# Two units of dense work moved ahead of transposes on TensorE in a two-block network

## What is computed

```
# first block, even layer
p   = modulate(x) @ w_in             # dq, dk, dv, gates, mk, mq, mo, mv
h_m = mlstm_mixer(...)               # scans over the gate rows, then h * sigmoid(o)
h_d = diff_mixer(...)                # 4 heads, softmax(s1) - lam * softmax(s2)
x   = x + gt_m * rmsnorm(concat(h_m, h_d) @ w_out)
x   = x + gt_f * rmsnorm(swiglu(modulate(x)))
# first block, odd layer
x   = x + gt_m * rmsnorm(conv_module(modulate(x)) @ pw2_w + pw2_b)
x   = x + gt_f * rmsnorm(moe_swiglu(modulate(x), router_w, w1, w3, w2))   # 8 experts, top 2
# second block, two layers
k, v = split(mem @ w_kv[i])          # the memory's keys and values
... gating / short conv, memory attention, w_out, layer norm, 16 experts in 4 groups
```

## Time and profile before

| | |
|---|---|
| median of 3 runs | 2243.79 us (2243.3, 2243.79, 2245.4) |
| profiled execution, its span on the page | 2243.4 us |
| PE busy | 2059.8 us (92%) |
| DVE, ACT, POOL busy | 496.3, 367.6, 116.4 us |
| share of the chain that ended last | PE 76%, DMA 11%, SPq 5%, DVE 4%, issue 2%, ACT 2% |
| read from memory | 641 MB, 286 GB/s over the span |

### The profile page before, as it was taken

One profiled execution on the slowest core, in us unless ns is written; L12 is line 12 of the kernel. 1 busy time (PEld: TensorE's weight loads), 2 busy tenths in 40 slices (PEclk: granted clock), 3 DMA queues, 4 the chain that ended last, 5 costly groups with the idle time before them and its releaser, 6 DMA issues.

```text
span 2243.4 us, 30002 instructions
## 1 busy us (share of the span) xinstructions
PE 2059.8 (92%) x12470; PEld 1004.1 (45%) x12470; DVE 496.3 (22%) x1255; ACT 367.6 (16%) x845; POOL 116.4 (5%) x275
## 2 busy tenths in 40 slices
PE   5989999999999989999999999959799978979995
PEld 2574547777677343322222222226443326643331
DVE  2143851000159320010000001021401113241113
ACT  2022432000332331000100010013111002111111
POOL 2000000000000100000000000000000000000010
PEclk9999999999999999999999999979899999979998
DMA  9241449442673578999999999982599995089995
GB/s 330 77 150 42 147 178 350 141 155 94 244 256 109 208 301 335 408 412 398 402 402 408 411 398 412 412 338 68 209 388 421 422 403 188 31 335 423 421 415 243
DMA packets 192025, 644.26 MB, mean 287 GB/s; under 512 B 11635, under 2 KB 44875, under 8 KB 156043
## 3 DMA queue, kind: packets, MB, share of 16 engines
q1 hardware_dynamic: 165440, 469.92, 55.0%
q0 software_dynamic: 25824, 172.09, 18.8%
q10 hardware_dynamic: 619, 0.23, 0.0%
HBM read 641.15 MB, written 1.05 MB: 286 GB/s over the span
## 4 chain that ended last, share of the span: by engine, by line
PE 76%; DMA 11%; SPq 5%; DVE 4%; issue 2%; ACT 2%; DVEq 0%; ACTq 0%; POOLq 0%
PE bank L1369 12%; PE bank L970 12%; PE bank L981 9%; PE bank L1406 9%; PE bank L1352 8%; PE bank L1277 7%; DMA ring<-in_l_moe_w 6%; SPq L762 5%; PE bank L1288 3%; DMA ring<-in_w_up 3%; PE bank L1325 3%; PE bank L1437 2%; PE bank L1594 1%; PE bank L1313 1%; DMA ring<-in_l_mod_w 1%
## 5 line engine op out<-in xcount | busy, mean ns | idle before, releaser
L1369 PE MATMUL bank<-ring,wide 128*32 128x512 f32 x3520 | 413.0, 599 | 23.8 <-DMA ring<-in_l_moe_w 22.1
L1406 PE MATMUL bank<-dreg,RB 128*32 128x512 f32 x2592 | 314.9, 605 | 9.5 <-DMA dreg<-in_l_moe_w 4.2
L1369 PEld LDWEIGHTS bank<-ring,wide 128*32 128x32 f32 x3520 | 108.5, 110 | 277.9 <-issue 247.9
L1352 PE MATMUL bank<-ring,wide 128*32 128x512 f32 x1408 | 173.8, 616 | 19.9 <-DMA ring<-in_w_up 18.5
L981 PE MATMUL bank<-wide,ring 128*128 128x256 f32 x832 | 183.5, 382 | 0.6 <-ACT wide L1856 0.6
L3005 DVE TENSOR_TENSOR H<-SG,bank 128x256 f32<-128x256 f32 x82 | 34.7, 423 | 659.3 <-ACT SG L2087 659.3
L981 PEld LDWEIGHTS bank<-wide,ring 128*128 128x128 f32 x832 | 159.0, 192 | 23.3 <-issue 1.3
L1406 PEld LDWEIGHTS bank<-dreg,RB 128*32 128x32 f32 x2592 | 79.6, 111 | 193.0 <-issue 184.5
L970 PE MATMUL bank<-ring,wide 128*128 128x512 f32 x352 | 157.1, 602 | 1.2 <-DMA ring<-in_w_kv 1.0
L1277 PE MATMUL bank<-wide,ring 128*128 128x256 f32 x704 | 153.6, 379 | 0.8 <-DVE MODX L2518 0.8
L1277 PEld LDWEIGHTS bank<-wide,ring 128*128 128x128 f32 x704 | 133.7, 190 | 23.0 <-issue 4.3
(11 more groups left out here) (444 smaller groups left out, 1608.8 us busy)
## 6 DMA issues: line engine op xcount, KB each, us to landing
ring<-in_l_moe_w SPq DMA_DIRECT2D x120, 1024.0 KB, 16.6
dreg<-in_l_moe_w POOLq DMA_DIRECT2D x88, 1024.0 KB, 8.6
dreg<-in_w_down POOLq DMA_DIRECT2D x64, 1024.0 KB, 12.0
ring<-in_w_gate SPq DMA_DIRECT2D x56, 1024.0 KB, 11.9
ring<-in_w_up SPq DMA_DIRECT2D x56, 1024.0 KB, 16.7
ring<-in_l_mod_w SPq DMA_DIRECT2D x24, 2048.0 KB, 8.4
ring<-in_l_moe_w SPq DMA_DIRECT2D x40, 768.0 KB, 12.3
ring<-in_l_ffn_w SPq DMA_DIRECT2D x22, 1024.0 KB, 10.4
```

The costliest lines, as they stand in the source:

```text
L1352: mm = pe.matmul(banks[r % 2][32 * g:32 * g + 32, :].rearrange("p (w n) -> p w n", w=2), tokens_of(m.order[i][0], c, k), w, start=k == 0, ...
L1369: mm = pe.matmul(banks[r % 3][32 * g:32 * g + 32, :].rearrange("p (w n) -> p w n", w=2), tokens_of(m.order[i][0], c, k), quads[:, s, :, k ...
L1406: mm = pe.matmul(banks[4 + 2 * m.lane(m.unit(m.order[i][0])) + h][32 * g:32 * g + 32, :], HQ[:, r % 4, j, 32 * q:32 * q + 32], dring[:, i ...
```

## The change

At the first place `unit_beside(0)`, which makes `mo0`, stands ahead of the wait for the gate rows and of their transposes. At the second, both modulation jobs stand first, then `kv1v1`, then the transposes of the tokens, and then both turns. The list of banks follows: `mo0` and `gT` change places, and so do `kv1v1` and the two turns. No instruction is added or removed.

```diff
-    names += ["dqT0", "dqT1", "dkT0", "dkT1", "gT"] + BESIDE[:1]
+    names += ["dqT0", "dqT1", "dkT0", "dkT1"] + BESIDE[:1] + ["gT"]
...
-    names += lagged(GAP5) + ["kv1v1", "part1", "rt1", "pos1", "cnt1"]
+    names += GAP5 + ["kv1v1"] + [f"{f}T" for f in GAP5] + ["part1", "rt1", "pos1", "cnt1"]
...
+            unit_beside(0)
             pe.wait_ge(sem("gate_rows"), 1)
             o = bank_for("gT")
             for s in range(4):
...
             filled(m, "gT")
-            unit_beside(0)
             pe.wait_ge(sem("diff_operands"), 1)
...
-            mod_jobs(GAP5)
+            for f in GAP5:
+                mod_job(f)
             tok_unit("kv1v1", memT, 1, w_kv)
             turn_normed(XN, 6)
+            for f in GAP5:
+                mod_turn(f)
```

More of the change, by code:

```diff
@@ L1116, in _ @@
                     filled(m, f"d{n}T{b}")
[L1118 to L1124, removed]
             beside = {}
@@ L1137, in _ @@
             unit_beside(0)
+            pe.wait_ge(sem("gate_rows"), 1)
+            o = bank_for("gT")
+            for s in range(4):
+                pe.transpose(o[:, s * GR:(s + 1) * GR], gG[:, s * P:(s + 1) * P], ident[0:GR, 0:GR])
+            for t in range(TT):
+                m = pe.transpose(o[:, (4 + t) * GR:(5 + t) * GR], gE[:, t * P:(t + 1) * P], ident[0:GR, 0:GR])
+            filled(m, "gT")
             pe.wait_ge(sem("diff_operands"), 1)
```

## The result

| | before | with the change |
|---|---|---|
| median | 2244.09 us (4 runs, 2243.3 to 2245.4) | 2230.52 us (4 runs, 2228.38 to 2232.55) |
| profiled execution, its span | 2243.4 us | 2226.8 us (its time 2228.38) |
| ratio | | 0.9931 [0.9919, 0.9943], or -15.5 us (-18.2 to -12.8) |

The kernel is faster by 0.6 to 0.7%. About 1.6 us of an execution's time lie outside its span (2228.38 less 2226.8). The spans differ by 16.6 us, more than the medians (13.6), since the execution shown of the change is its fastest, 2.1 us under its median, and that of before, with the same 1.6 us added to its span, would be at 2245.0, 0.9 above its own.

What follows compares the result with a forecast made beforehand. PE's own list was taken to bound the kernel to about 890 us, then expert loads until near 1460. Terms of 5.5 and 7.3 us made 12.8, so 2243.8 - 12.8 = 2231.0 us, range 2227.5 to 2236.5.

Steps and rivals of the forecast that it cites:

- Term 1: First mixer: `mo0` starts after ACT's first copy at full clock, so scores begin 5.5 us sooner (bounds 4.1 to 5.8).
- Term 2: Ahead of the experts: earlier `kv1v1` and token transposes, turns under ACT's evictions, save 7.3 us (bounds 6.8 to 7.7).
- The sum: Whole kernel: 5.5 + 7.3 = 12.8 us saved from the median of 2243.8 us, giving 2231.0 us.
- DVE and POOL: Ahead of the sort: DVE's gate rows end by 787.5, router's result near 788.7; POOL's constants keep some 2 us.
- The loads: Ahead of the experts: six loads on SP go at about 781.6 instead of 789.17 but land no sooner.
- Rival B: Ahead of the experts: late loads make PE stand until the old time, so 2238.3 us; 7%.
- D: Expert stage, 890 to 1460 us: changed load alternation lowers the DMA rate, time past 2248.3 us; 2%.
- E: Expert stage: a pace not set by PE loses the gain in part or whole, near 2243.8 us; 4%.
- Rival A: First mixer: the clock falls all the same, `mo0` takes 2.1 to 2.3 us more, 2233.3 us; 15%.
- Rival C: Gather ahead of the experts: its clock shifts, up to 3 us less (2228) or as much more (2234); 10%.

Runs made afterwards that it cites:

- both_again: The change once more, unaltered, beside runs of the kernel before: median 2232.08 us, ratio 0.9941.
- p1_only: The kernel before with only the first place changed (`mo0` ahead of the gate rows' transposes): 2239.91 us, ratio 0.9972.
- turns_first: The change with both modulation turns directly behind `kv1v1`, ahead of the tokens' transposes: 2232.90 us, ratio 0.9946 to before.
- turns_last: The change with both modulation turns behind the router instead of behind the tokens' transposes: 2235.79 us, ratio 0.9950 to before.
- p2_only: The kernel before with only the second place changed (`kv1v1` and the tokens' transposes ahead of both turns): 2237.51 us, ratio 0.9959.
- p2_filled: The kernel before with seven unused matmuls between the two modulation turns, no wait removed: 2243.99 us, ratio 0.9990.
- held: The change with unused matmuls in PE's waits, including ahead of `mo0`, their number cut to fit each wait: 2223.38 us, ratio 0.9903 to before.

## Why the prediction was right

The forecast was 2231.0 us; the medians of the change are 2230.52 and, in `both_again`, 2232.08.

- **Term 1**, 5.5 us forecast, 5.6 in the profile, and 6.3 (3.8 to 8.5) over the runs of `p1_only`. `mo0` was to start at 163.65 and started at 163.64: bank 1 did wait for ACT's first copy alone. The transposes behind it took 0.4 us and not 0.7, which is the 0.2 us that the scores (forecast 171.4, measured 171.17) came sooner.
- **Term 2**, 7.3 us forecast, 7.5 at the tokens' transposes and 7.1 at the first expert matmul, the difference being the gather's 7.11 us against 6.71. In PE's timeline the last router step starts 5.1 us behind the transposes' start (774.36 to 779.46), and so it did before (788.98 to 794.08): the turns lie wholly beneath ACT's evictions, and the 0.2 that the term allowed for them was not needed. The prediction lets half of `kv1v1` run at the lower clock before; by windows of the trace the clock was at half from 779.5 to about 782.9, which is 1.3 us of `kv1v1`. The sum doesn't use it. `turns_first` shows the cover by taking it away.
- **DVE and POOL.** DVE's room was put at some 1.2 us (787.5 to 788.7) and was 1.27. POOL's was put at "some 2 us" and is 2.0 to the sort; in `turns_last` it was DVE whose lateness the sort waited for.
- **The loads.** The six loads went out with the start of the tokens' transposes, in an unbroken row on SP:

```profile
774.55 47.68 SPq L762 DMA_DIRECT2D ring<-in_l_moe_w  x14
```

  They were asked for 14.6 us sooner than before (789.17), but the DMA engines were busy all along (share 1.00 to 1.03 in every window of 770 to 798) and ran out of work only near 799.7 (0.86 from 798 to 800), before near 807.2 (0.61 from 806 to 808). Those 7.5 us are about the lead of 7.1 with which the stage began, so in the times of the old trace these loads land hardly sooner, as forecast. PE waits for none of them at the first expert matmuls. Rival B fell, and D and E with it: the stage kept its length (701.5 against 702.0 us) and its rate.
- **Rival A** (15%) is real as a mechanism and rare: seen in the execution of `p1_only`, at 1.4 us, under the 2.1 to 2.3 that it was given. The clock fell ahead of `mo0` there too (0.76 from 164.5 to 165.0, 0.50 behind), but it was back in 168.0 to 168.5 (0.83), after 2.9 us of `mo0`; in the execution of before it was back in 171.5 to 172.0 (0.61), after 4.1. What the prediction said for and against this rival rests on a misreading. The 4.07 us of "issue" from 155.28 are a step of the chain at which DVE waited, not PE. PE's timeline and DVE's, of before:

```profile
154.78 4.48 PE L981 MATMUL bank<-wide,ring 128*128 128x256 f32 x20
```

```profile
159.36 0.88 DVE L2601 TENSOR_SCALAR wide<-bank,PCOL 128x256 f32<-128x256 f32 x2 [4.08 <-issue]
```

  PE started 20 matmuls in that time without a gap, so the clock at 1.00 in 155 to 159 says nothing of a wait, and PE had not "done little since 155.28". The Trainium skill ("TensorE: Matmul & The Clock Gate", Part 1) says that the window is free-running, so that the same kernel changes level at other moments; this agrees with an equal list that kept 1.00 in one execution and fell to 0.72 in another, the stretch being 1.65 us later, and with the two executions of the change itself at 580 us (1.00, and 0.50 in `both_again`).
- **Rival C** (10%) shows in the profiles, as part of the runs' spread. The gather took 7.11 us (the change), 6.97 (`both_again`), 6.72 (`turns_first`), 5.53 (`p2_only`) and 5.91 (`p2_filled`) with the same list at that point, and 3.78 with the clock held.
- **What the sum missed.** The spans differ by 16.6 us and not 12.8. At the first expert matmul the lead is 14.2 us: 5.6 and 7.1 from the two places, and 1.5 from the clock at the second mixer's transposes in the execution of before. The other 2.4 come later, where both kernels have the same lists. The lead is 14.7 at the fourth turn of the tokens. Another 1.2 come right behind it, once more from the clock: before, it was back only in 1515 to 1520 (0.83), 2.4 us into the unit that starts at 1514.30; in the change it was back as that unit began (1499.59; 0.54 from 1495 to 1500). The 0.5 up to the fourth turn and the last 0.7 are not traced. So 2.7 of the 3.8 us by which the spans beat the sum are luck of the two executions. Executions of one kernel differ by as much: 2228.4 to 2232.6 for the change, 2241.3 to 2248.9 over 27 runs of before. The medians differ by 13.6.
- **The base of the sum.** The prediction set the span of 2243.4 beside the median as if it were the execution's time; it lacks the 1.6 us around it. As the sum is a difference from the median, nothing followed from it.

## What to carry to other kernels

A wait of the matmul engine costs its length and then some at half clock behind it (here 1.6 and 2.4 us beside waits of 3.3 and 4.2), so a dense unit whose operands are ready belongs inside the wait, and small steps that another engine needs only later belong beneath that engine's evictions. Before moving them, count the room of whoever reads them next: 1.27 us of it were left on DVE, and one step further on cost 3.9. Where no useful work is ready, unused matmuls do a part of the job (2.4 of 5.6 us and 1.6 of 7.5 here), if they end before the wait does; each microsecond past that is paid. And a step called "issue" in a chain is to be looked up on the engine that it belongs to, with the branches of its list, before it is read as a wait of PE.

## What the hardware showed beyond that

- The clock can fall around a wait of only 1.00 us that follows another of 1.53 (`p1_only`: 0.72), and with the same list and waits it stayed up in seven other executions. The length of the wait alone doesn't tell which of the two happens.
- The gather (32 records of 128x96) takes 3.78 us at full clock and up to 7.11 at half. It stays at half though PE is almost always busy in it (3.97 of 4.00 us in 786 to 790, with its weight loads at 4.00); six unused matmuls ahead of it, 3.08 us of PE's time (2.40 and 0.68) that was a wait anyway, halve it.
- A branch can hold PE for microseconds. At L657 it takes PE 5.96 to 6.31 us ahead of the fourth and the sixth turn of the tokens in every kernel here, and DVE and ACT under 0.1 us. The third one, at the end of the program, takes PE 3.8 us in the change and 0.4 in `held`. Why it is so long on PE, no run here shows; it bounds what can be filled there.
